# Heads' sums of squares one step later in every layer, and the gated recurrence's running sums of log decays on VectorE instead of TensorE

## What is computed

```
q = rms_norm(q, gq)                                   # mean of squares over a head's 64 features
log_a = log_sigmoid(p_a @ gla_gate_up + gla_gate_bias) / 16
bcum = cumsum(log_a, axis=tokens)                     # within a chunk (128 tokens in the kernel)
```

## Time and profile before

| | |
|---|---|
| median of 3 runs | 2408.84 us |
| the profiled execution's own time | 2408.96 us |
| its span, first to last instruction | 2407.2 us |
| TensorE matmuls (PE) | 2369.0 us busy, 98% |
| VectorE (DVE) | 1326.1 us, 55% |
| ScalarE (ACT) | 930.7 us, 39% |
| GpSimd (POOL) | 152.6 us, 6% |
| granted TensorE clock | 1.000 |
| l2, its steps with attention | about 1075 to 1240 us of the span |

### The profile page before, as it was taken

How to read it: one execution, slowest core, us unless ns; L and a number is a source line. 1 busy time by engine, 2 the same in 40 slices (tenths; PEclk the granted TensorE clock), 3 DMA queues, 4 the chain that set the end, 5 groups by cost and what they waited for, 6 DMA issues and landing times.

```text
span 2407.2 us, 32810 instructions
## 1 busy us (share of the span) xinstructions
PE 2369.0 (98%) x13012; PEld 1921.2 (80%) x13012; DVE 1326.1 (55%) x1928; ACT 930.7 (39%) x1459; POOL 152.6 (6%) x197
## 2 busy tenths in 40 slices
PE   8999999999999999998999999999999999999999
PEld 6777777777888888876678888888888887888887
DVE  7666554787653433467765334356655556534433
ACT  5343463446342332446654223233332223422321
POOL 4001110000000000043220000000000000100000
PEclk9999999999999999999999999999999999999999
DMA  4222213222323333331023333222222212333322
GB/s 151 69 71 71 62 46 105 71 80 71 105 88 96 105 89 97 102 105 45 23 84 109 93 96 105 87 88 87 78 72 86 81 53 79 111 91 105 96 87 79
DMA packets 60639, 205.80 MB, mean 85 GB/s; under 512 B 7249, under 2 KB 7249, under 8 KB 60386
## 3 DMA queue, kind: packets, MB, share of 16 engines
q1 hardware_dynamic: 59760, 202.93, 28.0%
q10 hardware_dynamic: 754, 1.14, 0.2%
HBM read 201.94 MB, written 2.10 MB: 85 GB/s over the span
## 4 chain that ended last, share of the span: by engine, by line
PE 89%; DVE 6%; ACT 3%; issue 1%; POOL 1%; DMA 0%; SPq 0%; POOLq 0%; DVEq 0%; ACTq 0%
PE psum L1585 80%; ACT arena L757 1%; PE psum L1644 1%; PE psum L1610 1%; DVE ulo L1021 1%; PE psum L1740 1%; PE psum L1651 1%; PE psum L1693 1%; PE psum L1711 1%; PE psum L1619 1%; DVE stage L1012 0%; DVE arena L1250 0%; DVE cols L1256 0%; PE psum L1661 0%; PE psum L1657 0%
## 5 line engine op out<-in xcount | busy, mean ns | idle before, releaser
L1585 PE MATMUL psum<-hhi,whi 128*128 128x512 f32 x1640 | 647.2, 395 | 13.2 <-DVE wlo L979 10.0
L1585 PE MATMUL psum<-hlo,whi 128*128 128x512 f32 x1640 | 644.3, 393 | 0.0
L1585 PE MATMUL psum<-hhi,wlo 128*128 128x512 f32 x1640 | 643.9, 393 | 0.0
L1585 PE MATMUL psum<-uhi,whi 128*128 128x512 f32 x1392 | 548.0, 394 | 0.6 <-DVE arena L1057 0.6
L1585 PE MATMUL psum<-uhi,wlo 128*128 128x512 f32 x1392 | 545.5, 392 | 0.0
L1585 PE MATMUL psum<-ulo,whi 128*128 128x512 f32 x1392 | 544.5, 391 | 0.0
L979 DVE TENSOR_TENSOR wlo<-raw,whi 128x1024 fp32r<-128x1024 f32 (+1 forms) x399 | 465.9, 1168 | 65.9 <-ACT whi L651 33.9
L1585 PEld LDWEIGHTS psum<-hhi,whi 128*128 128x128 f32 x1640 | 308.5, 188 | 80.3 <-issue 12.2
L1585 PEld LDWEIGHTS psum<-hhi,wlo 128*128 128x128 f32 x1640 | 308.5, 188 | 64.7 <-issue 1.0
L1585 PEld LDWEIGHTS psum<-hlo,whi 128*128 128x128 f32 x1640 | 308.7, 188 | 63.4 <-issue 1.0
L944 ACT CAST whi<-raw 128x1024 fp32r<-128x1024 f32 x190 | 199.6, 1051 | 351.9 <-PE psum L1585 351.9
(11 more groups left out here) (231 smaller groups left out, 1757.1 us busy)
## 6 DMA issues: line engine op xcount, KB each, us to landing
raw<-in_packed_dram SPq DMA_DIRECT2D x359, 512.0 KB, 3.6
raw<-in_packed_dram SPq DMA_DIRECT2D x40, 256.0 KB, 2.6
x<-in_xt_dram SPq DMA_DIRECT2D x8, 256.0 KB, 7.2
out_dram<-x SPq DMA_DIRECT2D x8, 256.0 KB, 2.0
arena<-in_near_bias_dram ACTq DMA_DIRECT2D x1, 1024.0 KB, 6.3
vec<-in_vec_dram ACTq DMA_DIRECT2D x1, 44.0 KB, 4.3
arena<-in_gla_gate_up_dram ACTq DMA_DIRECT2D x1, 32.0 KB
arena<-in_gla_gate_bias_dram ACTq DMA_DIRECT2D x1, 2.0 KB
```

The source lines that it names most:

```text
L1585: mm = pe.matmul(g, w[:, u % 4, k, :], v[:, k, :], start=n == 0, stop=n == 3 * kt - 1)
```

## The change

Heads: the squares of a head unit are made at the end of the step after it, behind the step's parts, by ScalarE and by VectorE; the sums are made in the step after that, after 6 products; Ln, Exp and `post` follow there. If the unit between was a turn, its transposes come behind these sums in the same step and the same bank. ScalarE's and VectorE's `head` handling is put off as the gates' was. Recurrence: `lg(t)` swaps the operands, so that `lg(t)` has the 128 features of head `t` on partitions and all tokens free; VectorE makes four scans of 128 tokens each behind L1309; the triangle, its matmuls and ScalarE's four copies go. The steps of the first recurrence head keep no part but the last.

```diff
-    todo += zip(gla_head(0), [("decays", i) for i in range(5)] + [("gla", 0, -1)])
+    todo += zip(gla_head(0), [None] * 5 + [("gla", 0, -1)])
...
         def put_off(prev, u):
-            return prev is not None and units[prev][0] in GATES and not (units[u][0] == "copy" and units[u][5][0] == "gq")
+            if prev is None:
+                return False
+            gate = units[prev][0] in GATES and not (units[u][0] == "copy" and units[u][5][0] == "gq")
+            return gate or units[prev][0] == "head"
...
-            done(pool.memset(tri[:, :], 1.0))
-            done(pool.affine_select(out=tri[:, :], in_=tri[:, :], compare_op=ALU.is_ge, fill=0.0, base=0,
-                                    pattern=[[1, P]], channel_multiplier=-1))
...
-            def decays(i):
-
-                if i == 4:
-                    for h in range(4):
-                        act.wait_ge(gl_b_pe, 4)
-                        nc.scalar.copy(g_bs[:, h, :], psum[:, 2 + h, :]).then_inc(gl_b, 1)
...
                 for u, prev, parts in steps[name]:
-                    if prev is not None and units[prev][0] == "head":
-                        square_head(prev)
                     if u is not None:
                         split_hi(u + 2)
...
-                    if pending is not None:
+                    if pending is not None and units[pending][0] == "head":
+                        continue_with(pending)
+                    elif pending is not None:
                         gate(pending)
                     pending = prev if put_off(prev, u) else None
-                    if prev is not None:
+                    head = prev is not None and units[prev][0] == "head"
+                    if prev is not None and not head:
                         continue_with(prev)
...
                         gate(prev)
+                    if head:
+                        square_head(prev)
...
-                if u >= 2 and units[u - 2][0] in GATES:
+                if u >= 2 and units[u - 2][0] in GATES + ("head",):
                     dve.wait_ge(posted, u - 1)
...
                 dve.wait_ge(lg_ln, t + 1)
-                dve.scalar_tensor_tensor(out=g_lg[:, t, :], in0=psum[:, 2 + t, :], scalar=0.0, in1=g_z[t % 2],
-                                         op0=ALU.min, op1=ALU.subtract).then_inc(lg_done, 1)
+                l = g_z[t % 2]
+                dve.scalar_tensor_tensor(out=l, in0=psum[:, 2 + t, :], scalar=0.0, in1=l,
+                                         op0=ALU.min, op1=ALU.subtract).then_inc(lg_min, 1)
+                dve.wait_ge(lg_min, t + 1)
+                for c in range(NT):
+                    s = slice(P * c, P * c + P)
+                    ins = dve.tensor_tensor_scan(g_bs[:, t, s], ones[:, :], l[:, s], 0.0, ALU.mult, ALU.add)
+                ins.then_inc(lg_done, 1)
...
-                    if prev is not None and units[prev][0] == "head":
-                        square_head(prev)
...
+                    if before is not None and not head:
+                        post(before)
                     if parts and ahead(prev, parts[0]):
                         att(*parts[0][1:], "early")
                         parts = [parts[0] + ("late",)] + parts[1:]
-                    if before is not None:
+                    if before is not None and head:
                         post(before)
-                    if prev is not None and not late and not first_posted:
+                    if prev is not None and not late and not first_posted and not head:
                         post(prev)
                         squares_after(ORDER[name] + 1, prev - last)
                     for part in parts if not soon else []:
                         PARTS[part[0]](*part[1:])
                     if late and pending is None:
                         post(prev)
+                    if head:
+                        square_head(prev)
...
-                pe.matmul(psum[:, 2 + t, :], g_pa[0:17, P * t:P * t + P], g_up[0:17, :], start=True, stop=True).then_inc(lg_pe, 1)
+                pe.matmul(psum[:, 2 + t, :], g_up[0:17, P * t:P * t + P], g_pa[0:17, :], start=True, stop=True).then_inc(lg_pe, 1)
...
-                pe.wait_ge(lg_done, NT)
-                for c in range(NT):
-                    mm = pe.matmul(psum[:, 2 + h, P * c:P * c + P], g_lg[:, c, P * h:P * h + P], tri[:, :], start=True, stop=True)
-                mm.then_inc(gl_b_pe, 1)
...
-                    shared = [("shared_bank", prev)] * (prev in shared_before)
+                    shared = [("shared_bank", head)] * (head is not None)
+                    lead = 0 if soon else 6 if shared else 10
+                    if prev in TURNS:
+                        shared.append(("shared_bank", prev))
+                    head = prev if prev in HEADU else None
+                    lead = lead if shared else 0
                     between = parts + shared if soon else shared + parts
                     n = len(between) + 1
-                    lead = 0 if soon or not shared else 13 if units[prev][0] == "head" else 10
```

More of the change, by code:

```diff
@@ L318, in build @@
         g_head = [gla_head_places()]
-        g_lg = place(NT, 4 * P)
+        g_bs = place(4, SEQ)
         g_head.append(gla_head_places())
@@ L326, in build @@
         g_sq = [v for h in range(4) for v in g_head[h % 2][0:2]]
-        g_bs = g_lg.rearrange("p c (h k) -> p (c h k)", h=4).rearrange("p (h t) -> p h t", h=4)
         g_a = place(NT, P)
@@ L337, in build @@
         g_pa, g_up = g_kt.rearrange("p a b -> p (a b)"), g_a.rearrange("p a b -> p (a b)")
-        tri = sb("tri", [P, P])
         g_mask = sb("g_mask", [P, 6, 32])
@@ L342, in build @@
         up_in, pa_ones, lg_pe, lg_ln, lg_done = sem("up_in"), sem("pa_ones"), sem("lg_pe"), sem("lg_ln"), sem("lg_done")
-        gl_b_pe, gl_b, gl_d, gl_e, gl_f = sem("gl_b_pe"), sem("gl_b"), sem("gl_d"), sem("gl_e"), sem("gl_f")
+        lg_min, gl_d, gl_e, gl_f = sem("lg_min"), sem("gl_d"), sem("gl_e"), sem("gl_f")
         gl_level, gl_a, gl_kt_pe, gl_kt = sem("gl_level"), sem("gl_a"), sem("gl_kt_pe"), sem("gl_kt")
@@ L855, in nothing @@
                 pass
-            PARTS = {"ret": ret, "rates": rates, "att": att, "bias": bias, "lg": lg, "gla": gla, "decays": decays, "mask": nothing}
+            PARTS = {"ret": ret, "rates": rates, "att": att, "bias": bias, "lg": lg, "gla": gla, "mask": nothing}
             def static(name):
@@ L1352, in gla @@
                 if part == -1 and h == 0:
-                    dve.wait_ge(gl_b, 4)
+                    dve.wait_ge(lg_done, 4)
                 for what, n in {-1: ((difference, 0), (difference, 1)), 0: ((factors, 0), (difference, 2)),
@@ L1435, in bias @@
                 dve.wait_ge(dve_step, chain.up())
-            PARTS = {"ret": ret, "rates": rates, "att": att, "bias": bias, "lg": lg, "gla": gla, "mask": mask,
-                     "decays": lambda i: None}
+            PARTS = {"ret": ret, "rates": rates, "att": att, "bias": bias, "lg": lg, "gla": gla, "mask": mask}
             def static(name):
@@ L1449, in static @@
                     before, pending = pending, prev if put_off(prev, u) else None
-                    if before is not None:
+                    if before is not None and units[before][0] in GATES:
                         gate_logarithm(before)
@@ L1842, in gla @@
                     pe.matmul(MB, ones[:, :], g_sq[2 * h], start=True, stop=True).then_inc(gl_sum, 1)
-            def decays(h):
-                if h == 4:
-                    return
-                pe.wait_ge(lg_done, NT)
-                for c in range(NT):
-                    mm = pe.matmul(psum[:, 2 + h, P * c:P * c + P], g_lg[:, c, P * h:P * h + P], tri[:, :], start=True, stop=True)
-                mm.then_inc(gl_b_pe, 1)
             def nothing(*_):
                 pass
-            PARTS = {"ret": ret, "rates": nothing, "att": att, "bias": nothing, "lg": lg, "gla": gla, "decays": decays, "mask": mask,
+            PARTS = {"ret": ret, "rates": nothing, "att": att, "bias": nothing, "lg": lg, "gla": gla, "mask": mask,
                      "shared_bank": shared_bank}
@@ L1866, in static @@
             def static(name):
+                head = None
                 for u, prev, parts in steps[name]:
```

## The result

The changed kernel takes 2423.33 us (median of 5 runs, 2421.93 to 2425.59) against 2409.16 of the kernel before (5 runs): a ratio of 1.0058, 95% interval 1.0047 to 1.0070. It is slower, as forecast, but by 14.2 us and not by 7.2, and 2.3 us above the range. The profiled execution took 2425.59 us, span 2423.8, and is the slowest of the five; readings from it are some 2 us longer than the median.

A forecast was written before the change was run, and what follows sets the result against it. TensorE, busy 98% of the span, was taken to bound the kernel. Terms -11.7 + 6.7 + 1.2 + 10.6 - 3.2 + 3.6 = +7.2 on 2408.96 gave 2416.2, against the median 2416.0; whole range 2401 to 2421.

The forecast's parts named there:

- Heads in l1: Sums a step later in l1 find squares ready, -11.7 us; with new waits of +6.7 and +1.2, -3.8 in sum.
- (b): Heads after a softmax step in l1: squares queue behind softmax and exponentials, so sums wait 0 to 0.45 us, six times: +1.2.
- (a): Turns right behind a head in l1: transposes wait for the head's post to free bank XB, 5.85 plus 0.8 us: +6.7.
- Triangle: Recurrence: the triangle's four matmul bursts go, 0.80 us each: -3.2; ScalarE's copies bring nothing.
- Scans: VectorE's four scans delay the branch unit's post, so TensorE waits about 1.2 us for t = 0, 1 and 2: +3.6.
- low end of one element per cycle: Faster estimate for VectorE's scans: 0.20 us from start to start, four in 0.92 us, making the term +2.1.
- Heads in l2: Old stalls of 4.0 us go, but squares and posts queue in VectorE's and ScalarE's chain: +10.6, bounds +3 to +13.
- b0's key and turn: In l2, a longer chain before the turn's transposes leaves TensorE 5.9 us behind, including 1.6 from b0's query.
- key "a": In l2, posted 0.9 us later than other heads, so its turn waits 2.5 us; earlier masks pay for it.
- Slower still: Rival: l2's chain gives nothing back and scans take twice the slow form, 2422.4 us; chance 0.05.

The follow-up runs named there:

- Experiment 11: Changed kernel with late heads in l1 only, l1's transposes behind attention parts, and scans moved to four steps ahead of the first recurrence head: 2394.18 us.
- filled kernel: Changed kernel plus products nobody reads, put into l2's waits ahead of turns' transposes and some head sums: 2416.92 us.
- experiment 12: Kernel of Experiment 11 with the five heads of a in l2 late as well, b's heads staying early: 2398.15 us.
- experiment 5: Changed kernel with b's four queries in l2 summed early as before the change, b's keys and all heads of a still late: 2421.24 us.
- experiment 1: Changed kernel with the heads of both layers put back as before, the new recurrence kept: 2410.62 us against 2409.33 before.
- 10: Changed kernel with late heads in l1 only, and l1's transposes of turns right behind heads put behind the attention parts: 2399.08 us.
- 2: Changed kernel with head sums a step later in l1 alone, l2's heads as in the kernel before: 2404.24 us, 0.9980.

## Why the prediction was right in direction and wrong in size

- **Heads in l1: right but for (b).** Forecast -3.8, read -5.1. The waits named for (a) are there. By the units' starts the four steps cost +1.27, +2.35, +2.42 and +2.40; 0.45 of each is the two sums themselves, which the change moves into this step from another. What is left is 0.8 and 1.9 to 2.0 three times, 6.6 in place of (a)'s 6.7. The nine old stalls, by the starts around each in the kernel before, were 11.7 us, as I had them. What failed is (b), +1.2: no sum in l1 waits for a square any more. Without it the forecast is -5.0.
- **Triangle: right.** -3.7 against -3.2; a burst costs 0.92, not 0.80.
- **Scans: right.** Forecast +3.6, read 1.28 + 1.37 + 1.13 = 3.8 by the units' starts; four scans of 128 elements take 1.37 us. VectorE beside a branch unit:

```profile
353.64 0.69 DVE L1304 SCALAR_TENSOR_TENSOR arena<-psum,arena 128x512 f32<-128x512 f32 x1 [3.68 <-ACT arena L799]
...
354.37 1.37 DVE L1309 TENSOR_TENSOR_SCAN arena<-ones,arena 128x128 f32<-128x128 f32 x4
...
355.65 0.67 DVE L973 TENSOR_TENSOR wlo<-raw,whi 128x512 fp32r<-128x512 f32 x1
```

  The start of L973 comes 2.01 us behind that of L1304; before, L979 came 0.61 behind L1309: 1.40 us for four scans, where I had 1.36 from the slow form. Experiment 11 shows that this is a price of the place: moved, they cost nothing. The Trainium skill, page "DVE: opcode table, instruction layouts, handler registers and perf-mode slots", section "6. Datapath and trigger behaviour", has this scan at half throughput; 0.35 us from one scan's start to the next agrees, and the prediction's low end of one element per cycle (0.20 us a scan) is out.
- **Heads in l2: the step that failed.** "5.9 - 1.0 + 3.1 - 0.9 + 2.8 - 1.1 + 1.85 = 10.65: +10.6" counted the time that TensorE waits and took every product at 0.23 us, that is at full clock, behind waits of up to 3 us that it forecast itself. The runs showed products 0.43 us apart behind such waits. By the starts of the same units:

| stretch of l2 | forecast | filled kernel | changed kernel |
|---|---|---|---|
| a, up to b0's turn unit | 0 | +2.5 | +2.5 |
| b0's key and turn | +5.9 | +3.6 | +8.0 |
| up to b1's turn's step | +2.1 | +3.0 | +4.9 |
| up to b2's | +1.9 | +3.2 | +4.7 |
| up to b3's | +0.75 | +1.5 | +1.5 |
| sum | 10.65 | 13.8 | 21.6 |

  The last column less the one before it is the clock: 7.8 of the 10.95 us that I missed, 4.4 of them in b0's pair (in the first row both have one stretch at half clock, so its share is not split). Of the 7.0 us by which the medians missed the forecast, filling the waits gave 6.4 back. The other 3.2 are sizes: key "a" costs 2.5 where I had 0, since its turn waits 3.6 us from start to start and not 2.5, and only part of that is paid back (experiment 12 shows it by itself); b0 cost less than I had, b1 to b3 0.8 to 1.3 more each. The waits were the ones named, five of L1613 and those of the sums.
- **The rivals.** "Slower still", at 2422.4, came within 1 us of the median by luck: scans did not take twice the slow form, and the chain gave back 1.1, 0.6 and 1.2 us between pairs, nearly the 1.0, 0.9 and 1.1 that I had said. None of the rivals had a clock in it, although each wait of 2 to 3 us that I forecast was an idle TensorE in a kernel whose clock had been 1.00 in all of l2.
- **What stays open.** Why executions of one program lose the clock behind the same wait in some cases and not in others (experiment 5) was not found. Nor was it tried to give the sums a bank of their own in l2, which would part the transposes from the head's post; the kernel uses all eight there. That the queues, and not the bank, bind l2 is therefore argued and not shown.

## What to carry to other kernels

Putting an operation off by a step pays where the step has slack on the engines that feed it (l1) and costs where the step's other work queues ahead of it on the same engines (l2). When a change makes TensorE wait for some 2 us and more where it did not, price the products behind the wait too: here that was 7.8 us on top of 13.8 in the profiled executions, and 6.4 by the medians. The mean granted clock (0.995 in place of 1.000) gives it away, and a few products that nobody reads, put into the wait, tell the clock's share from the wait's.

## What the runs showed of the hardware

- TensorE's granted clock fell to its lower level, 1.2 GHz, for 3.4 to 6.8 us at a time in the changed kernel, behind waits of 1.8 to 3.6 us from start to start; products then started 0.43 us apart instead of 0.23. 50 further products of 128x512 in the waits brought all but one of five stretches back, and 6.4 us of the median.
- The same waits do not always bring it. Four executions of experiment 5 had mean clocks of 0.999 to 0.996 and took 2417.4 to 2424.1 us, that is about 2 us for 0.001 of the mean clock. A wait of 3.04 us at the head of l2 was followed by 6.8 us at half clock in experiment 1, by 3.4 in 10 and 11, and by none in 2. Nor did l1's waits for a post in the changed kernel bring it (2.1 us from start to start, three times), or two of 2.1 and 2.4 us at the head of l2 in the kernel before: the clock stood at 1.00 there.
- A scan of 128 elements takes 0.35 us of VectorE in a run of four, from start to start (0.40 from its start to its end), against 0.20 that the prediction estimated from plain rows for that many elements.
